# Loading each weight tile as two transfers of 64 partitions instead of two half rows of all 128

## The reference

```python
def swiglu(x, w_gate, w_up, w_down):
    return (jax.nn.silu(x @ w_gate) * (x @ w_up)) @ w_down

def reference(x, ...):
    for i in range(DEPTH):
        h = swiglu(x, ffn_w_gate[i, 0], ffn_w_up[i, 0], ffn_w_down[i, 0])
        x = layer_norm(ALPHA * x + 0.5 * h, ln_g[i, 0], ln_b[i, 0])
        j = i // N_MIXERS
        if i % N_MIXERS == 0:
            y = chunked_rel_attention(x, w_qkv_a[j], w_o_a[j], rel_bias)
        else:
            y = stick_breaking_attention(x, w_qkv_b[j], w_o_b[j])
        x = layer_norm(ALPHA * x + y, ln_g[i, 1], ln_b[i, 1])
        h = swiglu(x, ffn_w_gate[i, 1], ffn_w_up[i, 1], ffn_w_down[i, 1])
        x = layer_norm(ALPHA * x + 0.5 * h, ln_g[i, 2], ln_b[i, 2])
    return x
```

## Time and profile before

| | |
|---|---|
| Median of 3 runs | 980.01 us (979.96 to 980.14) |
| The profiled execution's own time | 979.89 us |
| Its span (first to last instruction) | 978.2 us |
| TensorE matmul busy | 965.3 us (99%) |
| DVE busy | 644.3 us (66%) |
| ACT busy | 487.3 us (50%) |
| Moved by DMA | 183.91 MB, a mean of 188 GB/s |
| Mean granted TensorE clock | 0.999 |

### The profile page before, as it was taken

The page is one execution under the profiler, slowest core; times in us unless marked ns, Lnnn a source line. Parts: engine busy times, 40 slices in busy tenths (PEclk is TensorE's granted clock), DMA queues, the critical chain, the costliest instruction groups (busy, mean ns, idle before and its releaser), DMA issues.

```text
span 978.2 us, 13347 instructions
## 1 busy us (share of the span) xinstructions
PE 965.3 (99%) x5196; PEld 812.9 (83%) x5196; DVE 644.3 (66%) x763; ACT 487.3 (50%) x605; POOL 42.0 (4%) x71
## 2 busy tenths in 40 slices
PE   8999999999999999999999999999999999999996
PEld 8888888887877888888888888888878788888885
DVE  5666673777567676664676666648777677666635
ACT  6555562356653555563245555443656445555530
POOL 0200000000101000000000000001111100000000
PEclk9999999999999999999999999999999999999999
DMA  9955566475452655557555556653744445555711
GB/s 354 310 180 203 176 212 232 159 254 164 155 172 90 234 193 182 200 179 255 172 174 192 193 179 200 242 190 128 239 155 157 145 148 196 182 200 176 234 68 44
DMA packets 51260, 183.91 MB, mean 188 GB/s; under 512 B 5872, under 2 KB 6032, under 8 KB 51216
## 3 DMA queue, kind: packets, MB, share of 16 engines
q1 hardware_dynamic: 48224, 174.08, 52.2%
q0 software_dynamic: 2560, 8.18, 2.6%
q10 hardware_dynamic: 432, 1.05, 0.3%
HBM read 182.21 MB, written 1.07 MB: 187 GB/s over the span
## 4 chain that ended last, share of the span: by engine, by line
PE 92%; DVE 2%; issue 2%; ACT 2%; DMA 1%; POOL 0%; SPq 0%; POOLq 0%; DVEq 0%; ACTq 0%
PE psum L373 30%; PE psum L377 15%; PE psum L325 11%; PE psum L326 11%; PE psum L327 11%; PE psum L505 5%; PE psum L508 2%; PE psum L545 1%; PE psum L555 1%; PE psum L313 1%; ACT w_hi L631 1%; DMA raw<-in_units 1%; PE psum L567 1%; ACT probs L744 0%; PE psum L394 0%
## 5 line engine op out<-in xcount | busy, mean ns | idle before, releaser
L828 DVE TENSOR_TENSOR w_lo<-raw,w_hi 128x2048 fp32r<-128x2048 f32 x162 | 369.2, 2291 | 192.7 <-ACT w_hi L631 192.4
L373 PE MATMUL psum<-xT,w_hi 128*128 128x512 f32 x1280 | 402.2, 396 | 0.0
L631 ACT ACTIVATE w_hi<-raw 128x2048 fp32r<-128x2048 f32 x162 | 307.3, 1908 | 98.5 <-PE psum L327 97.6
L377 PEld LDWEIGHTS psum<-xT,w_lo 128*128 128x128 f32 x1280 | 240.5, 188 | 56.8
L377 PE MATMUL psum<-xT,w_lo 128*128 128x256 f32 x1280 | 251.5, 278 | 0.0
L373 PEld LDWEIGHTS psum<-xT,w_hi 128*128 128x128 f32 x1280 | 195.1, 189 | 0.2
L325 PE MATMUL psum<-w_hi,hT_hi 128*128 128x512 f32 x416 | 163.3, 393 | 0.0
L327 PE MATMUL psum<-w_hi,hT_lo 128*128 128x512 f32 x416 | 162.0, 389 | 0.0
L326 PE MATMUL psum<-w_lo,hT_hi 128*128 128x512 f32 x416 | 162.0, 389 | 0.0
L676 ACT ACTIVATE hT_hi<-hiddenT 128x256 f32 (+1 forms) x82 | 34.3, 418 | 202.7 <-DVE hiddenT L857 202.7
L327 PEld LDWEIGHTS psum<-w_hi,hT_lo 128*128 128x128 f32 x416 | 78.1, 188 | 16.4
(11 more groups left out here) (77 smaller groups left out, 646.8 us busy)
## 6 DMA issues: line engine op xcount, KB each, us to landing
raw<-in_units SPq DMA_DIRECT2D x327, 512.0 KB, 4.7
gain<-in_ln_g POOLq DMA_DIRECT2D x6, 512.0 KB, 3.9
shift<-in_ln_b POOLq DMA_DIRECT2D x6, 512.0 KB, 5.1
x<-in_x SPq DMA_DIRECT2D x1, 1024.0 KB, 14.2
rel<-bias_by_distance POOLq DMA_DIRECT2D x8, 128.0 KB, 4.7
out<-x SPq DMA_DIRECT2D x4, 256.0 KB, 2.2
rel<-bias_by_distance POOLq DMA_DIRECT2D x8, 96.0 KB, 4.3
xT_raw<-in_xT ACTq DMA_DIRECT2D x2, 256.0 KB, 5.0
```

The source lines that it names most:

```text
L373: pe.matmul(TILE[j][:, which, :], as_gu(w_hi[s])[:, k, at:at + P], xT[:, kk, :, :], start=kk == 0, stop=False)
L377: last = pe.matmul(TILE[j][:, which, 0:SEQ], as_gu(w_lo[s])[:, k, at:at + P], xT[:, kk, 0, :], start=False, stop=kk == KD - 1)
L631: act.activation(w_hi[slot][:], raw[raw_slot][:], ACT.Copy).then_inc(hi_done, 1)
L828: dve.tensor_tensor(w_lo[slot][:], raw[raw_slot][:], w_hi[slot][:], ALU.subtract).then_inc(lo_done, 1)
```

## The change

A unit's two transfers are cut the other way. Before, each took half of the row (4 KB) of all 128 partitions. Now the first takes the whole row (8 KB) of partitions 0 to 63, and the second that of partitions 64 to 127. Each still moves 512 KB, and each still adds 16 to the same semaphore. The first two units, loaded by `load_first`, are not changed.

```diff
                 s = n % RAW
                 if n >= RAW:
                     slot_free(n)
-                for half in range(2):
-                    sp.dma_start(as_rows(raw[s])[:, half, :], as_rows(units[n])[:, half, :]
-                                 ).then_inc(raw_loaded[s], 16)
+                for rows in (slice(0, P // 2), slice(P // 2, P)):
+                    sp.dma_start(raw[s][rows, :], units[n, rows, :]).then_inc(raw_loaded[s], 16)
```

## The result

The changed kernel takes 987.5 us (median of 6 runs, 986.53 to 988.49) against 980.1 us (6 runs, 979.96 to 980.16): a ratio of 1.0077, 95% interval 1.0067 to 1.0087. The forecast was 988.0. The profiled run took 988.37 us for a span of 986.6; its span is 8.4 us longer than that of the kernel before. (In the new file the lines behind the change stand one lower: L372 is the old L373, L827 the old L828, L851 the old L852.)

What follows compares the result with a forecast made beforehand. TensorE was taken to bound the kernel, with loads scarce only in the start. Stalls of 1.9 + 2.3 + 1.9 + 2.0 = 8.1 us on 979.9 gave 988.0 us, whole range 981.5 to 996.

Steps and rivals of the forecast that it cites:

- The rate: Transfers into 64 partitions run at half the saturated rate: 205 GB/s, 5.1 us per unit in place of 2.56.
- The other half of the argument: At the loads: one queue works its transfers in order, so the second half can't fill in; part of taking 205 GB/s.
- The start: TensorE waits 1.9 us for unit 2, 2.3 for 3, 1.9 for 5, 2.0 among 6 to 9; all before 65 us.
- Unit 4 for unit 5: In the start: unit 4 costs nothing (split 34.5 us, wanted 35.2); unit 5 (split 39.9, wanted 38.0) costs 1.9 us.
- The norms' loads: GpSimd's `rel`, `gain` and `shift` loads, 1.5 MB, delay one odd unit, 7 or 9, by 3.7 us: 2.0 us of stall.
- The clock: Rival: the granted clock falls in the start's two stalls of about 2 us, adding 4 us, 992 us; 4%.
- The steady part: After the start, units are served in 5.1 us and used in 5.57; after 100 us landing takes 7 to 8 us, no cost.
- One sign: After 100 us ACT waits on no transfer; the prediction is wrong if waits on transfers go on past there.
- the 60 us forecast: The DMA engines stay saturated, share near 1, from the start to some 60 us.
- the rival of a bound throughout: Rival: loads bound the whole run at over 5.57 us per unit; 1,020 to 1,030 us at 6.2 us; 5%.

Runs made afterwards that it cites:

- even-odd run: Changed kernel, but each unit's two 64-partition transfers with 8 KB rows take the even partitions first, then the odd ones: 980.02 us, ratio 0.9999.
- transfer across partition 64: Changed kernel, but each unit by three transfers: partitions 32 to 95 first, then 0 to 31, then 96 to 127: 984.37 us, ratio 1.0044.
- run with `x` moved: Changed kernel with the 1 MB load of x issued behind unit 8 instead of behind unit 3: 987.03 us, ratio 1.0078.
- late-units run: Changed kernel, but only units 8 to 163 loaded in the new form, units 2 to 7 as in the kernel before: 979.94 us, ratio 1.0000.
- run with units 2 and 3: Changed kernel, but only units 2 and 3 loaded in the new form, the others as in the kernel before: 984.82 us, ratio 1.0051.

## Why the prediction was right, and where its steps were not

**The rate.** Half of 410 was forecast, 205 GB/s; measured 210 to 227. The Trainium skill (SBUF — State Buffer, "Door 1: The DMA port swizzle") names a reason, two groups of memory ports parted at partition 64. The even-odd run (422 GB/s) and the transfer across partition 64 (426 GB/s in the steady part) agree with it; the runs show no port itself. That half of the destination is open to a transfer at a time came out for 0 to 63 and 64 to 127, and not for other sets of 64. The other half of the argument, that the second half can't fill in because one queue works in order, was not tried by any run.

**The start.** Forecast 1.9 + 2.3 + 1.9 + 2.0 = 8.1 us of waiting. Measured 6.56 us, in other places: 1.07 us before 20 us (0.59 that was not there, and 1.33 against 0.79); 2.75 before unit 2; 0.70 before unit 3; 2.04 before unit 4. The 0.59 is for unit 1's last piece, which ACT could split from 13.91 us and not from 13.09; I had taken it to be untouched by the slow transfers queued behind it. The 1.33 is no loss, the first chunk started at 11.19 us and before at 11.15 (the even-odd run has 1.40 there and lost no time). Unit 2 landed at 18.6 us against 17.6, and the addition behind its split added 0.7, so its wait was 0.9 larger than forecast; unit 3's was 1.6 smaller, since it landed at 22.9 as forecast (22.6) and TensorE was already later.

**Unit 4 for unit 5.** The prediction gave unit 4 nothing (split at 34.5, wanted 35.2) and units 5, 7 or 9 another 3.9 us. The split of unit 4 was done at 35.78, and TensorE was out of work at 35.88 (37.92 - 2.04): by the split alone it would indeed have waited for nothing. It waited 2.04 us for the addition that comes behind the split, to 37.8. After that the even and the odd unit were in time. The step that failed is that a unit was held to be ready when its `w_lo` is: the small operations behind a late split are late by as much, and TensorE needs them too.

**The norms' loads.** Forecast 2.0 us; measured nothing. GpSimd issued them at 48.6 us, 12 us later than before (each of its two small loads took 8.0 us in place of 5.0 and 3.7), and by then, I take it, the delay had given the loads cover again; no run tries this alone. In the run with `x` moved, where TensorE was on unit 4 earlier, it did wait for loads at 72 and 84 us.

**The clock.** Given 4%, and it happened, though behind the third wait and not in the first two: 1.7 us, with 0.90 and 0.68 of the clock over 36 to 44 us. That and the waiting that was forecast and did not come nearly cancel: 8.1 forecast, 8.4 in the profiled run, 7.4 between the medians. That the total came out so near is in part luck; it was better than its parts.

**The steady part.** As forecast: issue to landing 7.4 us, no cost; the late-units run alone gives 1.0000. One sign did not hold: the prediction wanted no wait of ACT on a transfer after 100 us and called itself wrong if there were any. There are four, at 153, 449, 634 and 931 us, 0.9 to 1.2 us each. TensorE doesn't notice, so the sign was too strict and the cost is still nothing; where these waits come from was not followed. The engines also stayed full for longer than the 60 us forecast (a share of 0.95 from 70 to 130 us). The queue's share rose to 78.6%, not to twice 52.2%, and TensorE lost nothing behind 60 us, which rules out the rival of a bound throughout.

## What to carry to other kernels

Cut a load so that each transfer's partitions lie on both sides of partition 64, and the transfers queued beside it too (the run with 32 to 95 first gained little while they mixed); how long its rows are mattered nothing here, and neither did one transfer or two. A load that is hidden in the steady part can be the bound in the first tens of microseconds: price a slower transfer there, unit by unit, with every small operation that stands behind the late one and that the engine also needs, and not only the tile itself. A megabyte moved out of a bound stretch has to land in one that has cover.

## What the runs showed that I had not expected

- Partitions 0 to 63 and then 64 to 127: 220 GB/s. Even and then odd ones: 422 GB/s, for the same sizes and number of transfers.
- Partitions 32 to 95 as one transfer, in the steady part: 426 GB/s. Queued back to back with transfers of one side: 227 to 257.
- An upper half on ACT's queue beside pieces of all 128 partitions on SP's: 227 GB/s for both together.
- The granted clock fell to 1.2 GHz (0.50 from 24 to 25 us in the run with units 2 and 3) after TensorE had waited 2.70 us, once; in the changed kernel it held at 1.00 after a wait of 2.75 us and fell after a later one of 2.04 us. Executions of the slower kernels also spread by 1.1 to 3.4 us, where those of the kernel before spread by 0.2 to 0.7; that the clock is the reason was not shown.
